# A decoder layer with a product-key expert mixer: tokens in two chunks, the second's dense layer written between the first's expert steps

## The chip, the cores and the metric

One core of one Trainium2 chip. The metric is the device time of one launch in microseconds, from runs of the whole kernel. "Span" is the time from the first to the last instruction in a profiled execution.

## The reference, cut to what matters

520 tokens (a prompt of 512 and 8 sample rows) pass one layer of width 1024. Its dense part is a conditioned norm, a recurrent branch (RG-LRU) beside windowed attention, a gated merge and a projection. Behind it stands the expert mixer: per token, 8 heads pick 16 of 16384 experts each, and for each expert one row of `u_tab` is dotted with the token and one row of `v_tab` is added with a weight.

```python
def layer(x, c, pos, conv_buf, h0, attn_fn, lp):
    ...
    hn = modulate(rmsnorm(x, lp['g_norm1']), sh1, sc1)
    z = hn @ lp['w_in']
    ...
    merged = jax.nn.sigmoid(gate_r) * y_r + jax.nn.sigmoid(gate_a) * y_a
    x1 = x + gt1[:, None, :] * (merged @ lp['w_out'])
    h2 = modulate(rmsnorm(x1, lp['g_norm2']), sh2, sc2)
    x2 = x1 + gt2[:, None, :] * peer(h2, lp['w_pq'], lp['sub_keys'], lp['u_tab'], lp['v_tab'])

def peer(h, w_pq, sub_keys, u_tab, v_tab):
    ...
        u = jnp.take(u_tab, ec, axis=0)
        act = jax.nn.gelu(jnp.einsum('cd,ced->ce', hc, u).astype(jnp.float32), approximate=False)
        wgt = (gc * act).astype(hc.dtype)
        vr = jnp.take(v_tab, ec, axis=0)
        return jnp.einsum('ce,ced->cd', wgt, vr)
```

A row of either table is 1024 float32, 4 KB. 128 tokens x 128 experts x 4 tiles, twice, and one group more for the sample rows: 65 groups of 8 u and 8 v gathers, each of 128 rows.

## The kernel before, in words

Each engine has its own program; semaphores order them, and each engine works through its program in order. There are two parts, one after the other.

**The dense layer** runs over all 520 tokens, as two halves of 260 columns (`HALF`). TensorE works off a list of "products" (`_plan`, L85 to L149), each into one of four accumulators of two PSUM banks. Most weights come in units of 1 MB into a ring of three (`load`, L406, on SP's queue). A weight block of 128 columns is used as a pair: ScalarE rounds it (`split_until`, L794), GpSimd subtracts to get the rest (L1460), and `project_split` (L505 to L515) does three matmuls for each piece of the contraction, 48 for a block: 24 for each half. Two rounded blocks fit at a time (`NHI`), so a rounding waits for the product two before it to end. `modulation` (L522 to L529) takes 24 units of 1 MB with 9 columns. The recurrence, the softmax and the merges stand on VectorE and ScalarE between them. At the end `keys` (L699 to L713) gives the scores for the experts.

**The experts** follow. VectorE's `topk` (L1332) finds a head's 16 indices and weights. A group is one half of a head, eight experts for each of 128 tokens, 64 groups (`GROUPS`) and one for the sample rows. For each group GpSimd issues eight gathers from `u_tab` and then eight from `v_tab` (`group`, L1446 to L1454), each of 128 rows into one of eight buffers; a u gather waits until VectorE has read the buffer (`s_urd`), a v gather until TensorE has (`s_vrd`). VectorE dots each u row with the token (`dot_products`, L1392 to L1397), ScalarE makes eight diagonal matrices of the weights (`weights`, L985 to L997), and TensorE adds up the v rows with them (`expert_sums`, L717 to L724). Tiles and heads are hardware loops (`Fori`). GpSimd's first gather waits until its last weight block is split, and VectorE, TensorE and ScalarE start on the experts once the dense layer is done. After each tile `finish` (L1399) adds the residual and norms the row.

Of the kernel before, what the change touches and what calls it, by code (L numbers as in the profile page):

```python
# [18 lines left out]
HALF = N // 2  # L29
# [18 lines left out]
SLOT = 8  # L48

# [22 lines left out]
RING = 3  # L72
UNIT = 2 * DC * P
NHI = 2
SPLIT = ("xr", "gr", "qk", "v", "gate_r", "gate_a", "attn", "out", "pq")
NACC = 4
STEPS = TILES * NKV
SAMPLE_STAGE = {0: 1, 2: 2, 3: 3}
UNIT_COLS = {"mod": UNIT, "xr": UNIT, "gr": UNIT, "band": 6 * P, "qk": UNIT, "v": UNIT, "gate_r": UNIT, "rnn": RC * P,
             "gate_a": UNIT, "attn": UNIT, "out": UNIT, "pq": UNIT, "keys": PH * NKEYS}  # L80
UNIT_NO, PRODUCT_NO, UNIT_READ = {}, {}, []
SPLIT_NO = {}


def _plan():  # L85
    def unit(name, i, *products):
        UNIT_NO[name, i] = len(UNIT_READ)
        UNIT_READ.append(0)
        if name in SPLIT:
            SPLIT_NO[name, 2 * i] = len(SPLIT_NO)  # L90
            SPLIT_NO[name, 2 * i + 1] = len(SPLIT_NO)
        for p in products:
            product(*p)
            UNIT_READ[-1] = len(PRODUCT_NO)

    def product(name, i=0, reads=None):
        PRODUCT_NO[name, i] = len(PRODUCT_NO)
        if reads:
            UNIT_READ[UNIT_NO[reads]] = len(PRODUCT_NO)

    for i in range(8):
        unit("mod", i, ("mod", i))
        if i == 3:
            product("norm", 0)
    for name, m in (("xr", 8), ("gr", 13)):
        for i in range(RC // 2):
            unit(name, i, (name, 2 * i), (name, 2 * i + 1))
            unit("mod", m + i, ("mod", m + i))
    for i in range(RC):
        unit("band", i, ("band", 2 * i), ("band", 2 * i + 1))  # L110
    for i in range(RC // 2):
        unit("qk", i, ("qk", 2 * i), ("qk", 2 * i + 1))
        unit("mod", 18 + i, ("mod", 18 + i))
        if i:
            product("turn", 2 * i - 2)
            product("turn", 2 * i - 1)
    unit("v", 0, ("v", 0), ("turn", RC - 2), ("turn", RC - 1), *[("v", t) for t in range(1, TILES + 1)])
    product("s", 0)
    product("sample", 0)
    unit("mod", 23, ("mod", 23))  # L120
    for i in range(STEPS):
        product("t", i)
        if i + 1 < STEPS:
            product("s", i + 1)
        if i in SAMPLE_STAGE:
            product("sample", SAMPLE_STAGE[i])
        product("o", i)
        c = i // 2
        if i % 4 == 0:
            unit("gate_r", c // 2)  # L130
        if i % 2 == 0:
            product("gate_r", c, ("gate_r", c // 2))
        else:
            unit("rnn", c, ("rnn", c))
    for i in range(DC // 2):
        unit("gate_a", i, ("gate_a", 2 * i), ("gate_a", 2 * i + 1))
        unit("attn", i, ("attn", 2 * i), ("attn", 2 * i + 1))
    for i in range(DC // 2):
        unit("out", i, ("out", 2 * i), ("out", 2 * i + 1))
    product("norm", 1)  # L140
    for i in range(2 * (TILES + 1)):
        product("rows", i)
    product("spread")
    for q in range(2):
        for i in range(4 * q, 4 * q + 4):
            unit("pq", i, ("pq", 2 * i), ("pq", 2 * i + 1))
        unit("keys", q, *[("keys", 2 * t + q) for t in range(TILES + 1)])
    for name, i in (("gt2", 0), ("gt2", 1), ("y", 0)):
        product(name, i)  # L149
# [40 lines left out]
def peer_program(nc, X, Wd, O):  # L190
    ctx = ExitStack()
    with ctx:
# [563 lines left out]
        def _(act):  # L756
# [51 lines left out]
            def two(a):  # L808
                return a[:, :, 0:HALF]
# [794 lines left out]
```

## Time and profile before

| | |
|---|---|
| runs, median of 3 | 2475.72 us (2469.61 to 2476.45) |
| profiled execution, span | 2483.4 us |
| busy, share of the span | TensorE 77%, VectorE 51%, ScalarE 28%, GpSimd 52% |
| first u gather issued | 903.87 us |
| u gathers / v gathers | 520 / 520 |
| moved by GpSimd's queue | 545.33 MB |
| moved by the other queue | 89.24 MB |

The profiled execution's own time is its span; no other time of it is given. Busy shares are means over two parts with different limits, so the parts are read apart. A busy TensorE means that matmuls are under way, not that they run at their peak.

### The profile page before, as it was taken

What the parts mean: (1) busy time and instruction counts of PE and PEld (TensorE: products, weight loads), DVE (VectorE), ACT (ScalarE), POOL (GpSimd) and SP (SyncE); (2) the same over time, 40 slices, a digit from 0 to 9 for tenths busy, and PEclk for the clock granted to TensorE, in tenths of its full rate; (3) what the DMA queues carried; (4) which work ended last, traced back from release to release, by engine and by line L of the source; (5) the groups of instructions that cost most, each with busy time, mean ns of one, the idle gap of its engine ahead of it and who ended that gap; (6) DMA issues with size and microseconds to landing.
All of it is one profiled execution on the core that took longest, in us unless ns stands there. A gap on an engine that the chain in (4) does not pass through costs nothing.

```text
span 2483.4 us, 25659 instructions
## 1 busy us (share of the span) xinstructions
PE 1922.2 (77%) x8102; PEld 1260.9 (51%) x8102; DVE 1273.5 (51%) x2896; ACT 706.2 (28%) x1770; POOL 1287.2 (52%) x1126
## 2 busy tenths in 40 slices
PE   8899988999997986676667757757767666776676
PEld 8899888888997972232223323323223222332232
DVE  2430366434333107656656746655756655765663
ACT  1222422233223323323313323222313323323222
POOL 0221123001431346667676766767767667766663
PEclk8899988999998997888878878788888888878877
DMA  5233332112221238999999999999999998999996
GB/s 222 94 131 111 123 136 97 39 47 82 86 86 35 77 134 334 366 363 360 362 332 357 373 342 363 361 339 340 366 356 358 354 351 327 369 354 358 372 347 233
DMA packets 164900, 635.52 MB, mean 256 GB/s; under 512 B 18800, under 2 KB 19640, under 8 KB 156224
## 3 DMA queue, kind: packets, MB, share of 16 engines
q0 software_dynamic: 149760, 545.33, 58.7%
q1 hardware_dynamic: 15072, 89.24, 10.1%
q8 instruction: 49, 0.80, 0.1%
q14 instruction: 19, 0.16, 0.0%
HBM read 631.30 MB, written 5.20 MB: 256 GB/s over the span
## 4 chain that ended last, share of the span: by engine, by line
PE 41%; issue 19%; DVE 15%; POOL 8%; DMA 6%; another core or an unknown queue 5%; ACT 5%; POOLq 0%; DVEq 0%; ACTq 0%; SPq 0%
PE acc L722 9%; POOL arena L1443 8%; PE acc L512 6%; PE acc L513 6%; PE acc L514 6%; DVE arena L1396 6%; DMA arena<-in_u_tab,pku 5%; PE acc L528 4%; PE acc L496 3%; ACT arena L996 2%; PE acc L562 2%; ACT pk L991 1%; PE acc L631 1%; PE acc L649 1%
## 5 line engine op out<-in xcount | busy, mean ns | idle before, releaser
L722 PE MATMUL acc<-arena 128*128 128x512 f32 x2080 | 1048.5, 668 | 473.6 <-ACT arena L996 346.8
L722 PEld LDWEIGHTS acc<-arena 128*128 128x128 f32 x2080 | 442.8, 217 | 1080.7 <-issue 1078.9
L1396 DVE CUSTOM_DVE_ANT_0 arena<-arena 128x1024 f32<-128x1024 f32 x520 | 631.2, 1226 | 416.0 <-DMA arena<-in_u_tab,pku 378.4
L1443 POOL DMA_INDIRECT arena<-in_v_tab,pku x520 | 552.9, 1063 | 316.3 <-issue 157.6
L1443 POOL DMA_INDIRECT arena<-in_u_tab,pku x520 | 526.2, 1012 | 167.3 <-issue 152.2
L1460 POOL TENSOR_TENSOR w_lo<-arena,w_hi 128x1024 fp32r<-128x1024 f32 x80 | 194.6, 2437 | 682.1 <-ACT w_hi L794 682.1
L512 PE MATMUL acc<-h_hi,w_hi 128*128 128x260 f32 x992 | 292.7, 295 | 22.0 <-DVE h_lo L1101 11.7
L513 PE MATMUL acc<-h_lo,w_hi 128*128 128x260 f32 x992 | 287.9, 290 | 0.0
L514 PE MATMUL acc<-h_hi,w_lo 128*128 128x260 f32 x992 | 287.1, 289 | 0.0
L988 ACT ACTIVATE pk<-pk 128x8 f32<-128x8 f32 x65 | 13.6, 209 | 936.3 <-issue 617.6
L512 PEld LDWEIGHTS acc<-h_hi,w_hi 128*128 128x128 f32 x992 | 194.4, 196 | 25.7 <-DVE h_lo L1101 12.6
L513 PEld LDWEIGHTS acc<-h_lo,w_hi 128*128 128x128 f32 x992 | 194.3, 196 | 2.0 <-issue 1.9
L514 PEld LDWEIGHTS acc<-h_hi,w_lo 128*128 128x128 f32 x992 | 194.2, 196 | 0.0
L794 ACT CAST w_hi<-arena 128x1024 fp32r<-128x1024 f32 x80 | 83.1, 1048 | 358.1 <-PE acc L514 325.4
L996 ACT ACTIVATE arena<-const,pk 128x128 f32<-128x128 f32 x520 | 158.8, 387 | 7.1
L528 PE MATMUL acc<-small,arena 128*128 128x9 f32 x768 | 111.6, 288 | 6.4 <-DMA arena<-w_mod 6.4
L528 PEld LDWEIGHTS acc<-small,arena 128*128 128x128 f32 x768 | 112.0, 236 | 6.4 <-issue 6.3
L991 ACT ACTIVATE pk<-pk 128x1 f32<-128x1 f32 x520 | 103.6, 281 | 2.1
L1349 DVE MAX8 pk<-arena 128x8 f32<-128x128 f32 x132 | 38.8, 294 | 76.7 <-ACT arena L966 53.9
L496 PE MATMUL acc<-arena 128*128 128x260 f32 x320 | 72.0, 385 | 0.0
L496 PEld LDWEIGHTS acc<-arena 128*128 128x128 f32 x320 | 61.4, 192 | 13.4 <-issue 4.4
L1077 DVE TENSOR_TENSOR mod<-acc,par 128x18 f32<-128x18 f32 x24 | 4.0, 176 | 116.7 <-PE acc L528 116.4
(230 smaller groups left out, 1863.0 us busy)
## 6 DMA issues: line engine op xcount, KB each, us to landing
arena<-w_mod SPq DMA_DIRECT2D x24, 1024.0 KB, 4.9
arena<-in_u_tab,pku POOLq DMA_INDIRECT x520
arena<-in_v_tab,pku POOLq DMA_INDIRECT x520
arena<-w_pq SPq DMA_DIRECT2D x8, 1024.0 KB, 4.7
arena<-w_xr SPq DMA_DIRECT2D x5, 1024.0 KB, 4.9
arena<-w_gr SPq DMA_DIRECT2D x5, 1024.0 KB, 4.9
arena<-w_qk SPq DMA_DIRECT2D x5, 1024.0 KB, 4.7
arena<-w_rnn SPq DMA_DIRECT2D x8, 640.0 KB, 4.0
```

Of the source, the lines that this page charges most:

```text
L496: mm = pe.matmul(a[:, h, 0:HALF], w[:, k, :], rhs[:, k, h * HALF:(h + 1) * HALF], start=(k == 0), stop=(k == ks - 1))
L512: pe.matmul(a[:, h, 0:HALF], w1[:, k, :], hi[k][:, cols], start=(k == 0), stop=False)
L513: pe.matmul(a[:, h, 0:HALF], w1[:, k, :], lo[k][:, cols], start=False, stop=False)
L514: mm = pe.matmul(a[:, h, 0:HALF], w2[:, k, :], hi[k][:, cols], start=False, stop=(k == DC - 1))
L528: mm = pe.matmul(a[:, c, 0:NCOND], w[:, c, k, :], cond[:, k, :], start=(k == 0), stop=(k == DC - 1))
L722: mm = pe.matmul(y[:, h, :], diag[q][:, j, :], vt_row[j][:, h * 512:(h + 1) * 512], start=False, stop=True, skip_group_check=True)
L794: act.copy(w_hi[n % NHI], half_unit(name_n, c_n)).then_inc(s_hi, 1)
L991: ins = act.activation(wcol[q][:, j:j + 1], gl[:, j:j + 1], ACT.Copy, scale=g[:, j:j + 1])
L996: ins = act.activation(diag[q][:, j, :], basis, ACT.Copy, scale=wcol[q][:, j:j + 1])
L1396: dve.tensor_tensor_reduce(u_row[j], u_row[j], hcur, 1.0, 0.0, ALU.mult, ALU.add, dots[q][:, j:j + 1]).then_inc(s_urd, 1)
L1443: pool.indirect_dma_start(out=row, out_offset=None, in_=table, in_offset=bass.IndirectOffsetOnAxis(ap=idx, axis=0), **more).then_inc(signa ...
L1460: pool.tensor_tensor(lo, half_unit(name, c), hi.bitcast(F32), ALU.subtract).then_inc(s_lo, 1)
```

## The change

Tokens come in two chunks, 256 and 264 columns (256 and the 8 sample rows). The first chunk's dense layer runs alone up to its first `keys` product (`PEER_FROM`). From there the kernel goes in 66 steps: step g holds VectorE's dots of group g and TensorE's sums of group g - 1. Each step has four quarters (`PARTS`). What is left of the dense work is cut into pieces by planned costs, one piece behind each quarter of steps 0 to 34 (`_limits`): 381.5 us of planned cost in steps 0 to 29, 32.2 in steps 30 to 34; 413.2 lie before `PEER_FROM`. Every engine's dense program is a generator that is run up to the quarter's limit (`Course`). All weights but the modulation's are loaded and split once for each chunk, in pieces of 128 columns; four piece buffers and two rounded ones serve the second chunk (eight and four before the first v gather, whose buffers they borrow). Accumulators are six of one bank, and the expert sums have a pair to themselves. Rows and scores of both chunks pass through DRAM (`spill`), loaded again by SP when a step wants them. Loops over tiles and heads are written out. Indices and weights have three buffers, and a head's choice stands two groups ahead.

GpSimd's order in a step is eight u gathers of group g, eight v gathers of group g - 1, then all weight splits of the step. `ROUND_AT` names for each weight block the product whose end lets ScalarE round it; GpSimd's split follows. In steps 1 to 29 the last such product lies in the fourth quarter except in steps 13, 16, 18 and 20 (third), 11, 14, 19, 26 and 29 (second) and 5 (none); in steps 30 to 32 in the fourth, in 33 and 34 there is none.

```diff
+CT = 2
+CP = CT * P
+W = CP + NB
+TOK = (CP, W)
...
+OWN, EXTRA = 4, 4
+OWN_HI, EXTRA_HI = 2, 2
+NACC = 6
...
+    def split(ch, name, c):
+        product(ch, name, c, ((name, c),), 2.9)
...
+PEER_FROM = NO[0, "keys", 0] + 1
...
+        over = max(free[p], HI_AFTER[p])
+        m = min([m for m in points if m + 1 >= over]) if n >= OWN_HI + EXTRA_HI else -1
...
+PARTS = 4
+HALF_WAY = NO[1, "keys", KEYS_B - 1] + 1
+HALF_STEP = 2 * PH * CT - 2
+LAST_STEP = HALF_STEP + 5
...
+    for (lo, hi), steps in (((PEER_FROM, HALF_WAY), HALF_STEP), ((HALF_WAY, NPRODUCTS), LAST_STEP - HALF_STEP)):
+        total, spent, at = sum(COST[lo:hi]), 0.0, lo
+        for i in range(steps * PARTS):
+            goal = total * (i + 1) / (steps * PARTS)
+            while at < hi and spent + COST[at] / 2 <= goal:
+                spent += COST[at]
+                at += 1
+            limits.append(hi if i == steps * PARTS - 1 else at)
...
+        class Course:
...
+            def until(self, limit):
+                while self.at < limit:
+                    self.at = next(self.steps, NPRODUCTS)
...
         @block.tensor
...
+            def expert_sums(g, js):
...
+                if js[0] == 0:
+                    pe.wait_ge(s_diag, g + 1)
...
+                for j in js:
+                    pe.wait_ge(s_vt[j], 16 * (g + 1))
...
+            course = Course(dense())
+            course.until(PEER_FROM)
+            for g in range(GROUPS + 2):
+                for q in range(PARTS):
+                    if g:
+                        expert_sums(g - 1, (2 * q, 2 * q + 1))
+                    if g * PARTS + q < len(LIMITS):
+                        course.until(LIMITS[g * PARTS + q])
...
         @block.scalar
...
+            def round_pieces(product):
...
+                while split[0] < len(SPLITS) and ROUND_AT[split[0]] <= product:
+                    piece = SPLITS[split[0]]
+                    src = await_piece(act, piece)
+                    if HI_AFTER[piece]:
+                        act.wait_ge(s_ready, HI_AFTER[piece])
+                    act.copy(w_hi[HI_SLOT[piece]], src[:, 0:D]).then_inc(s_hi, 1)
...
+            for g in range(GROUPS + 2):
...
+                if g:
+                    weights(g - 1)
+                for q in range(PARTS):
...
+                    if g * PARTS + q < len(LIMITS):
+                        course.until(LIMITS[g * PARTS + q])
...
         @block.vector
...
+            for g in range(GROUPS + 2):
+                tile, step = divmod(g - 1, 2 * PH)
+                for q in range(PARTS):
+                    if g <= GROUPS:
+                        dot_products(g, (2 * q, 2 * q + 1))
...
+                    if q == 1 and g % 2 == 0 and g // 2 + 1 <= HEADS:
+                        choose(g // 2 + 1)
...
+                    if g * PARTS + q < len(LIMITS):
+                        course.until(LIMITS[g * PARTS + q])
...
         @block.gpsimd
...
+            def gather_u(g, j):
...
+                if g:
+                    pool.wait_ge(s_urd, SLOT * (g - 1) + j + 1)
+                gather(u_row[j], X["u_tab"], indices(g, j), s_u[j], {})
...
+            def gather_v(g, j):
...
+                else:
+                    pool.wait_ge(s_vrd, SLOT * (g - 1) + j + 1)
...
+            def dense():
+                for n, p in enumerate(SPLITS):
+                    yield max(ROUND_AT[n], 0)
+                    hi, lo = w_hi[HI_SLOT[p]], w_lo[PIECE_SLOT[p]]
+                    pool.wait_ge(s_hi, n + 1)
+                    pool.tensor_tensor(lo, ring[PIECE_SLOT[p]][:, 0:D], hi.bitcast(F32), ALU.subtract).then_inc(s_lo, 1)
...
+            for g in range(GROUPS + 2):
+                if g <= GROUPS:
+                    for j in range(SLOT):
+                        gather_u(g, j)
+                if g:
+                    for j in range(SLOT):
+                        gather_v(g - 1, j)
+                for q in range(PARTS):
+                    if g * PARTS + q < len(LIMITS):
+                        course.until(LIMITS[g * PARTS + q])
```

## Rows read from the trace of the kernel before

**Rows 1.** The page, busy tenths of the span in 40 slices of 62 us.

```profile
PE   8899988999997986676667757757767666776676
...
DMA  5233332112221238999999999999999998999996
...
GB/s 222 94 131 111 123 136 97 39 47 82 86 86 35 77 134 334 366 363 360 362 332 357 373 342 363 361 339 340 366 356 358 354 351 327 369 354 358 372 347 233
```

**Rows 2.** Windows: us; busy of PE, PEld, DVE, ACT, POOL; PEclk, DMA, GB/s.

```profile
616.00:709.00 93.00, 91.33 (x760) 91.12 (x758) 39.02 (x47) 20.84 (x24) 37.81 (x16) 1.00 0.27 92
...
903.00:2460.00 1557.00, 1063.51 (x2177) 454.40 (x2178) 963.36 (x2249) 443.22 (x1325) 1079.12 (x1040) 0.83 0.94 352
...
1050.00:1100.00 50.00, 33.64 (x64) 14.05 (x64) 30.61 (x71) 14.46 (x52) 33.59 (x35) 0.79 0.97 375
...
1700.00:1750.00 50.00, 37.13 (x73) 15.86 (x73) 32.97 (x82) 15.21 (x45) 34.62 (x32) 0.83 0.91 333
```

**Rows 3.** Timeline of POOL at the first gathers: start us, us, what, idle before.

```profile
903.87 1.11 POOL L1443 DMA_INDIRECT arena<-in_u_tab,pku  x1 [9.00 <-DVE carrier L1388]
...
912.74 0.93 POOL L1443 DMA_INDIRECT arena<-in_u_tab,pku  x1 [0.31 <-issue]
...
921.14 0.94 POOL L1443 DMA_INDIRECT arena<-in_v_tab,pku  x1 [7.46 <-PE acc L728]
```

**Rows 4.** Timeline of the last group and the last store.

```profile
2434.06 0.93 POOL L1443 DMA_INDIRECT arena<-in_u_tab,pku  x1 [0.31 <-issue]
...
2481.21 0.32 SPq L471 DMA_DIRECT2D out_ys<-arena  x1
```

**Rows 5.** Timeline of DVE, a head's first and last index step.

```profile
850.27 0.29 DVE L1349 MAX8 pk<-arena 128x8 f32<-128x128 f32 x1 [53.92 <-ACT arena L966]
...
859.96 0.17 DVE L1376 CAST pku<-pk 128x16 uint32<-128x16 f32 x1
```

**Rows 6.** The chain that ended last: start us, us, what.

```profile
70.22 4.89 DVE h_lo L1101 x8
...
88.61 3.47 PE acc L528 x32
...
409.98 6.63 PE acc L603 x32
...
1160.46 5.25 DMA arena<-in_v_tab,pku
...
986.90 6.40 DMA arena<-in_u_tab,pku
...
1771.38 7.43 DMA arena<-in_u_tab,pku
```

**Rows 7.** Timeline of PE, two groups of expert sums.

```profile
1323.85 16.14 PE L722 MATMUL acc<-arena 128*128 128x512 f32 x32 [7.77 <-remote]
...
2459.80 14.79 PE L722 MATMUL acc<-arena 128*128 128x512 f32 x32 [0.23 <-ACT arena L996]
```

**Rows 8.** Timeline of ACT and POOL, one weight piece rounded and split.

```profile
620.88 1.05 ACT L794 CAST w_hi<-arena 128x1024 fp32r<-128x1024 f32 x1 [7.73 <-PE acc L514]
...
622.01 2.39 POOL L1460 TENSOR_TENSOR w_lo<-arena,w_hi 128x1024 fp32r<-128x1024 f32 x1 [9.24 <-ACT w_hi L794]
```

**Rows 9.** Timeline of ACT and PE, from a group's dots to its sums.

```profile
1342.26 0.21 ACT L988 ACTIVATE pk<-pk 128x8 f32<-128x8 f32 x1 [11.89 <-DVE pk L1396]
...
1344.20 2.44 ACT L996 ACTIVATE arena<-const,pk 128x128 f32<-128x128 f32 x8
...
1346.78 3.78 PE L722 MATMUL acc<-arena 128*128 128x512 f32 x4 [6.79 <-ACT arena L996]
```

**Rows 10.** The page, a DMA queue (packets, MB, share) and an issue group.

```profile
q1 hardware_dynamic: 15072, 89.24, 10.1%
...
arena<-w_mod SPq DMA_DIRECT2D x24, 1024.0 KB, 4.9
```

**Rows 11.** Timeline of POOL, a gather that took twice as long.

```profile
931.70 1.99 POOL L1443 DMA_INDIRECT arena<-in_u_tab,pku  x1 [0.30 <-issue]
```

More of the change, by code:

```diff
@@ L454, in _ @@
[L454 to L467 removed]
+            order = list(PIECES)
@@ new lines, in dense @@
+            def dense():
+                pe.wait_ge(s_cond, 1)
+                for i in range(8):
+                    yield NO[0, "mod", i]
+                    modulation(i)
+                    if i == 3:
+                        yield NO[0, "norm", 0]
+                        first_norm(0)
+                for ch in range(2):
+                    yield from chunk(ch)
+            def expert_sums(g, js):
+                tile, part, first, last = group_of(g)
+                if js[0] == 0:
+                    pe.wait_ge(s_diag, g + 1)
+                    if first and tile:
+                        pe.wait_ge(s_yfree, tile)
+                for j in js:
+                    pe.wait_ge(s_vt[j], 16 * (g + 1))
@@ new lines, in dense @@
+            def dense():
+                act.wait_ge(s_c, 16)
+                act.activation(cond, cT, ACT.Sigmoid).then_inc(s_sig0, 1)
+                act.wait_ge(s_par, 16)
+                first_norm_squares(0)
+                act.wait_ge(s_lam, 1)
+                act.activation(lamt[:, 1, :], lamt[:, 0, :], ACT.Exp, scale=-1.0).then_inc(s_elam, 1)
+                yield NO[0, "norm", 0]
+                root(0, 0)
+                for ch in range(2):
+                    yield from chunk(ch)
@@ new lines, in dense @@
+            def dense():
+                link(dve.memset(st_conv, 0.0))
+                dve.wait_ge(s_c, 16)
+                dve.wait_ge(s_sig0, 1)
+                dve.tensor_tensor(cond, cond, cT, ALU.mult).then_inc(s_cond, 1)
+                dve.wait_ge(s_par, 16)
+                decay_rates()
+                for i in range(4):
+                    yield NO[0, "mod", i]
+                    modulation(i)
+                yield NO[0, "norm", 0]
+                scale_rows(0, 0, xT, xT, rstd)
+                for i in range(4, 8):
+                    yield NO[0, "mod", i]
+                    modulation(i)
+                for i in range(8 - NACC, 8):
+                    await_read(dve, 0, "mod", i)
+                gains(0, prm("g1"))
+                modulate(0, 0, xT)
+                for ch in range(2):
+                    yield from chunk(ch)
@@ L1439, in _, with settled, gather @@
+            final_norm(TILES - 1)
+            add_residual(TILES)
+            final_norm(TILES)
         @block.gpsimd
         def _(pool):
-            def gather(row, table, idx, signal, read=None):
-                more = {} if read is None else {"engine_sem": read}
+            def settled():
+                pool.sem_inc(s_passed, 1)
+            def gather(row, table, idx, signal, more):
+                settled()
                 pool.indirect_dma_start(out=row, out_offset=None, in_=table,
@@ L1467, in _, with indices @@
[L1467 to L1475 removed]
+            def indices(g, j):
+                if g == GROUPS:
+                    return eidx_s[:, j:j + 1]
+                col = g % 2 * SLOT + j
+                return eidx[g // 2 % 3][:, col:col + 1]
@@ L1479 @@
+            course = Course(dense())
+            course.until(PEER_FROM)
+            for g in range(GROUPS + 2):
[5 more added lines that the diff above has]
+                        gather_v(g - 1, j)
+                for q in range(PARTS):
+                    if g * PARTS + q < len(LIMITS):
+                        course.until(LIMITS[g * PARTS + q])
 def kernel(**inputs):
```

2319 lines of the change are left out of this document (1318 added, 1001 removed).

## The prediction

> **What bounds the kernel now.** I read the page's busy tenths first: the span has two halves. Up to slice 14 TensorE is at 8 or 9 tenths and the DMA engines mostly idle; from slice 15 the DMA engines are at 9 and TensorE at 6 or 7 [rows 1]. The windows give sizes: in the dense layer TensorE is busy 91.3 of 93 us, in the experts the DMA engines are busy 0.94 of the time at 352 GB/s [rows 2]. The dense half runs to the first gather at 903.9 [rows 3], and 64 groups of 16 gathers begin between there and 2434.1 [rows 4], one in 23.91 us; the last takes 49.3 more to the end at 2483.4. A group is 16 x 128 rows of 4 KB, 8.39 MB, so its floor is 22.4 us at the best rate shown, 375 GB/s, and 25.2 at the worst, 333 [rows 2]. Laying the idle DMA under the busy TensorE is thus worth looking for: half the dense layer beside half the experts.
>
> **What the change adds up to.** I split the new order in four: first chunk alone, steps that hold dense work, plain steps, tail.
>
> *First chunk alone.* Before, dense products begin at 75.1, when the last rest is written [rows 6]; the first chunk's rows are half as wide, so I take 70. From 75 to 903.9 are 828.8 us, with 16 modulation units of 3.47 [rows 6], 55.5 in all; 773 are left, half of which is 387. Of this the second half of pq now comes after the first gather: 8 products of 24 matmuls at 91.33/760 = 0.120 us [rows 2], 23 us. The modulation comes back whole, 55.5, and a head's choice of indices costs 860.1 - 850.3 = 9.9 [rows 5]. 70 + 387 - 23 + 55.5 + 9.9 = 499; the sample rows' attention, one piece of which is 6.6 [rows 6], goes with the second chunk, so I take 490. The ends: 455 if only the plan's costs count (413 to that point, with the idle of the start), 530 if every gap is paid whole.
>
> *The chain of a step with dense work.* GpSimd's program in step g is: eight u of group g, eight v of group g - 1, then every weight split that the plan puts in step g. A split waits for ScalarE's rounding, which waits for a product to end that TensorE works off in step g, and TensorE puts two rows' sums of group g - 1 ahead of each quarter's products. So the v rows of group g cannot be asked for until TensorE is nearly through step g, and TensorE cannot begin step g + 1 until they land. From GpSimd's start of a step:
> - eight u gathers at (912.74 - 903.87)/7 = 1.27 us each [rows 3], then the first v is issued at 10. It lands 5.25 to 7.43 us after its issue, with a full queue [rows 6]: at 15.3 to 17.4. I take 16.
> - TensorE: eight rows of sums take 16.1 us after 7.8 us of idling, 14.8 after a short gap [rows 7]. It will have idled longer than 7.8, so I take 16.1. Dense products beside them: the plan's 381.5 us over 30 steps, 12.7 a step; its 2.9 for a product agrees with 24 x 0.120 = 2.88 [rows 2]. Together 28.8.
> - the last split: the cast begins at 620.88, the split ends at 624.40 [rows 8], 3.5; with a signal and the next issue, 3.9.
>
> Sum: 16 + 28.8 + 3.9 = 48.7 us when the last rounding of the step hangs on a product of its last quarter. From the plan's limits and rounding points, written out, that is so in 19 of steps 1 to 29. In four (13, 16, 18, 20) it hangs on the third quarter, 3.4 + 3.2 earlier: 42.1. In six it hangs on the second or there is none; then ScalarE sets the period, since the weights of the next group stand behind its dense work: an eviction of 0.6, a table load of 1.3 and 1342.26 to 1346.78 = 4.5 [rows 9] behind TensorE's 28.8: 35.2. Steps 30 to 34 hold 6.4 us of dense: three of 16 + 22.5 + 3.9 = 42.4, two of 22.5 + 6.4 = 28.9. Together 19 x 48.7 + 4 x 42.1 + 6 x 35.2 + 3 x 42.4 + 2 x 28.9 = 1490. Step 0 has no v and waits for u, dots and a choice: 20.
>
> VectorE's additions (dots twice two, a choice of 9.9 every second step, its dense pieces) fill some 20 us of such a step and lie beside TensorE. SP's queue carries the second chunk's weights and the spilled rows: at most 89.2 MB less the 25.2 of modulation [rows 10], 64 MB, 1.9 per step, 5 us of DMA time that falls where the gathers have drained. Both cost nothing as long as the step is this long. If the cover goes, those 5 us join the step: 170 in all, which would only add to a step that is already long. The loops written out and the accumulators of one bank instead of two I put at nothing; no row prices them, and what they can give is bounded by the 1.5 us by which a plain step of before exceeds its floor, what they can cost by the first chunk's range.
>
> A gather into an empty queue has no row here. The Trainium skill (DMA: Bandwidth & Descriptors, Anatomy of one DMA) puts a GpSimd DMA at 2.0 us plus its bytes at 436 GB/s, 3.2 us for such a row, as an estimate; the rows above say 5.25 at the least. By the page the v rows would land 2 us earlier in some 30 steps, and the sum would be 60 us lower.
>
> *Plain steps and tail.* Steps 35 to 63 have no splits; u and v gathers queue behind each other as before, 29 x 23.91 = 693, between 22.4 and 25.2 each [rows 2]. The last group and the end: 49.3. Together 743.
>
> 490 + 20 + 1490 + 743 = 2743 of span, against 2483.4. That span lies 7.7 above the median of the runs shown, 2475.72; I take the 7.7 off: **2735**, slower by 10.5%. In short, 34 dense steps of 43.8 us cost more than 34 plain steps and the dense work in a row: 34 x 23.91 + 414 = 1227.
>
> Own range: the landing of v, 1.2 either way in 26 steps, 31; sums at 14.8, 44 less; first chunk 35 less or 40 more; plain steps 43 less or 38 more; attention steps 10 to 15, where VectorE's choice stands ahead of a softmax, up to 60 more. Not all at one end: 2600 to 2870.
>
> **Rivals.**
> - *The last split never sets the step* (faster). If splits come out early everywhere, each step is TensorE's 28.8 with ScalarE's 6.4: 29 x 35.2 + 5 x 28.9 = 1165, so 490 + 20 + 1165 + 743 - 8 = 2410. For it: six steps are like that already. Against: GpSimd's order leaves no way round. It decides from a mean step of (2483.4 - 490 - 20 - 743)/34 = 36.2 us downward. Chance 0.10.
> - *Full overlap, the DMA engines bound* (faster): (8.39 + 1.9)/0.352 = 29.2 a step, 993 for 34, in all 2238. For it: DMA idles in the dense half. Against: the same order, and TensorE alone needs 28.8. Chance 0.05.
> - *No overlap at all*: the products run in gaps, 1227 for the 34 steps, in all 2472; no change that can be told. Chance 0.04.
> - *GpSimd's head of a step is slow*: gathers of 1.99 us beside VectorE's work do occur, against 0.94 [rows 11, 4]. At 1.99 + 0.3 the first v is issued at 18.3 instead of 10; 8.3 us in 26 steps is 216: 2950. Against: in the 1557 us of the experts GpSimd was busy 1079 for 1040 gathers [rows 2], 1.04 each, so few are slow. The Trainium skill (SBUF — State Buffer, SBUF: two separate sides) has VectorE's two-port copies lock GpSimd out of writing descriptors, and the second chunk brings such copies beside the gathers. Chance 0.08.
>
> **How the numbers follow.** The forecast's mechanism has 0.73. A measurement of this kernel tells about 0.3% from no change, 7 us. Slower by more: 0.73 + 0.08, less a little for the near end, 0.80. Faster: 0.10 + 0.05 and a share of the in-a-row case, 0.17. Same: 0.03. The range leaves out the faster cases and the far part of the slow head: 2580 to 2910.
>
> **What would show it.** Right: in the dense steps, u gathers bunch right behind a split and the DMA share falls to near 0.5 to 0.65 there, with TensorE idle some 16 us behind each bunch, waiting for a v row; steps of 40 to 49 us up to step 30 and near 24 from step 35; first gather near 490. Wrong in the chain: v rows already landed when TensorE begins its sums, steps of 29 to 36 us, DMA share over 0.85. Wrong in size: a first gather beyond 530, gathers near 2 us, or TensorE waiting for softmax rows in steps 10 to 15.

## The result and the profile after

The changed kernel takes 3040.55 us (median of four runs, 3024.30 to 3049.53) against 2472.66 of the kernel before beside it: a ratio of 1.2286, interval 1.2240 to 1.2331. Slower, as forecast, but by more than twice as much: 2735 was given, with 2910 as the upper end. The profiled execution has a span of 3047.7 us. Line numbers below are those of the changed kernel.

The page of the changed kernel: busy tenths in 40 slices of 76 us, one DMA queue (packets, MB, share), and groups of instructions (busy us, mean ns, idle time before them and what ended most of it).

```profile
PE   7978997364665555564657474664666666565666
...
DMA  5444453556755645646565656576789888888886
...
q1 hardware_dynamic: 53136, 158.16, 15.5%
...
L1031 PE MATMUL y<-arena 128*128 128x512 f32 x2080 | 1068.9, 671 | 996.3 <-DMA arena<-in_v_tab,pku 932.8
...
L1890 POOL TENSOR_TENSOR w_lo<-arena,w_hi 128x1024 fp32r<-128x1024 f32 x160 | 386.2, 2416 | 1018.6 <-ACT w_hi L1064 1018.6
...
L1858 POOL DMA_INDIRECT arena<-in_u_tab,pku x520 | 581.0, 1117 | 317.8 <-DVE pk L1749 158.9
```

In [rows 1] one of the two was at 8 or 9 tenths nearly everywhere. Here, from slice 9 to 28, TensorE is at 4 to 7 tenths and the DMA engines at 4 to 7 as well. TensorE and GpSimd, which issues the gathers, wait for each other: over the whole span TensorE idles 996 us ahead of the expert sums, 933 of them ended by v rows, and GpSimd idles 1019 us ahead of splits, all for ScalarE's rounding (653 and 647 of these in steps 1 to 34, as lines further down show). The second chunk fetches the weights again: 158 MB on SP's queue against 89 in [rows 10].

Windows of the changed kernel: us, busy of PE, PEld, DVE, ACT and POOL, granted clock, DMA share, GB/s. They are the first chunk from 100 us on, steps 1 to 34, and steps 35 to 63.

```profile
100.00:547.60 447.60, 386.54 (x2582) 366.61 (x2581) 175.75 (x388) 179.87 (x337) 162.43 (x70) 0.87 0.44 145
577.50:2201.20 1623.70, 932.78 (x3930) 599.62 (x3930) 694.37 (x1579) 405.20 (x1029) 786.18 (x630) 0.78 0.61 216
2201.20:2983.30 782.10, 478.46 (x984) 204.64 (x985) 424.02 (x1035) 185.14 (x601) 512.11 (x465) 0.80 0.86 319
```

The same view of the kernel before, its dense layer from 100 us on.

```profile
100.00:904.00 804.00, 760.73 (x5430) 718.67 (x5429) 274.53 (x568) 238.38 (x416) 198.66 (x79) 0.94 0.24 86
```

From the issue of each step's first u gather the span divides as the forecast's sum did:

| term | forecast, us | measured, us | more |
|---|---|---|---|
| first gather | 490 | 547.6 | 58 |
| step 0 | 20 | 30.0 | 10 |
| 34 steps with dense work | 1490 | 1623.7 | 134 |
| 29 plain steps | 693 | 782.1 | 89 |
| last group to the end | 49.3 | 64.4 | 15 |
| span | 2743 | 3047.7 | 305 |

The timeline of the changed kernel: the first gather; step 24, from its first u gather to that of step 25, on all engines; then a pair of plain steps (43 and 44). Columns: start, us, what, idle before and what ended it.

```profile
547.57 1.09 POOL L1858 DMA_INDIRECT arena<-in_u_tab,pku  x1 [11.41 <-DVE pku L1795]
...
1733.11 0.97 POOL L1858 DMA_INDIRECT arena<-in_u_tab,pku  x1 [0.15 <-issue]
...
1743.61 0.94 POOL L1858 DMA_INDIRECT arena<-in_v_tab,pku  x1 [0.30 <-issue]
...
1749.99 5.66 PE L1031 MATMUL y<-arena 128*128 128x512 f32 x8 [20.61 <-DMA arena<-in_v_tab,pku]
...
1778.55 1.04 ACT L1064 CAST w_hi<-arena 128x1024 fp32r<-128x1024 f32 x1 [4.37 <-PE acc L749]
...
1779.67 2.34 POOL L1890 TENSOR_TENSOR w_lo<-arena,w_hi 128x1024 fp32r<-128x1024 f32 x1 [4.78 <-ACT w_hi L1064]
...
1782.15 0.95 POOL L1858 DMA_INDIRECT arena<-in_u_tab,pku  x1
...
2421.46 0.94 POOL L1858 DMA_INDIRECT arena<-in_u_tab,pku  x1 [0.30 <-issue]
...
2429.29 0.17 DVE L1795 CAST pku<-pk 128x16 uint32<-128x16 f32 x1
2429.37 1.22 DVE L1749 CUSTOM_DVE_ANT_0 arena<-arena 128x1024 f32<-128x1024 f32 x1
...
2431.41 1.14 POOL L1858 DMA_INDIRECT arena<-in_u_tab,pku  x1 [9.01 <-DVE pk L1749]
2432.85 1.99 POOL L1858 DMA_INDIRECT arena<-in_u_tab,pku  x1 [0.30 <-issue]
```

Step 24 is the forecast's chain, link by link: eight u issues (10.5 us), the v row 6.4 after its issue, TensorE idle for 20.6 until then, 28.6 to the last rounding, 3.6 to the next step's first u. In all 49.0 us, against the forecast's 16 + 28.8 + 3.9 = 48.7.

The plain steps show something that the forecast did not have. In step 43 GpSimd issues four u gathers and then stands for 9.0 us. It waits for dot product 4 of the even step before, whose row it is to overwrite, and that dot product stands behind the choice of the next head's indices, whose last step is the row at 2429.29. In the kernel before GpSimd's order was the same, eight u and then eight v, but the choice stood behind all eight dot products of a group; the last of them and the first row of the choice:

```profile
1739.17 1.23 DVE L1396 CUSTOM_DVE_ANT_0 arena<-arena 128x1024 f32<-128x1024 f32 x1
...
1740.32 0.29 DVE L1349 MAX8 pk<-arena 128x8 f32<-128x128 f32 x1
```

The change put it between dot products 3 and 4. So the steps alternate: the 15 odd ones take 33.2 us on average, the 14 even ones 20.3, in the mean 26.97 where the kernel before takes 23.91, and the DMA share is 0.86 instead of 0.94 [rows 2].

### The profile page after: what moved, and what is told of

The parts are those of the page before. It is cut to its first block, busy times and chain, and to the rows that moved or that the text cites. A ratio compares the mean times of both kernels' runs of the same rounds, so it can differ in the third digit from the quotient of the medians.

```text
span 3047.7 us, 25065 instructions
## 1 busy us (share of the span) xinstructions
PE 1934.2 (63%) x8078; PEld 1279.1 (42%) x8078; DVE 1349.7 (44%) x3142; ACT 807.5 (26%) x2040; POOL 1513.2 (50%) x1206
## 3 DMA queue, kind: packets, MB, share of 16 engines
q0 software_dynamic: 149760, 545.33, 48.7%
q8 instruction: 64, 1.05, 0.1%
## 4 chain that ended last, share of the span: by engine, by line
issue 23%; PE 15%; DVE 13%; DMA 8%; POOL 8%; another core or an unknown queue 4%; ACT 2%; POOLq 0%; DVEq 0%; ACTq 0%
PE y L1031 10%; POOL arena L1858 6%; DVE arena L1749 5%; DMA arena<-in_v_tab,pku 5%; DMA arena<-in_u_tab,pku 3%; POOL w_lo L1890 2%; PE acc L749 1%; PE acc L747 1%; PE acc L748 1%; DVE pku L1770 1%; DVE pk L1778 1%; DVE pku L1779 1%; DVE pk L1769 1%; ACT w_hi L1064 1%
## 5 line engine op out<-in xcount | busy, mean ns | idle before, releaser
L1031 PE MATMUL y<-arena 128*128 128x512 f32 x2080 | 1068.9, 671 | 996.3 <-DMA arena<-in_v_tab,pku 932.8
L1031 PEld LDWEIGHTS y<-arena 128*128 128x128 f32 x2080 | 440.7, 218 | 1545.4 <-issue 1491.9
L1890 POOL TENSOR_TENSOR w_lo<-arena,w_hi 128x1024 fp32r<-128x1024 f32 x160 | 386.2, 2416 | 1018.6 <-ACT w_hi L1064 1018.6
L1858 POOL DMA_INDIRECT arena<-in_u_tab,pku x520 | 581.0, 1117 | 317.8 <-DVE pk L1749 158.9
L1064 ACT CAST w_hi<-arena 128x1024 fp32r<-128x1024 f32 x160 | 167.2, 1046 | 1042.1 <-PE acc L749 696.4
L747 PE MATMUL acc<-h_hi,w_hi 128*128 128x256 f32 (+1 forms) x992 | 319.5, 322 | 14.8 <-DVE h_lo L1420 14.8
L749 PE MATMUL acc<-h_hi,w_lo 128*128 128x256 f32 (+1 forms) x992 | 288.4, 291 | 0.7 <-issue 0.7
L748 PE MATMUL acc<-h_lo,w_hi 128*128 128x256 f32 (+1 forms) x992 | 288.6, 291 | 0.0
L1296 ACT ACTIVATE pk<-pk 128x16 f32<-128x16 f32 x33 | 10.1, 307 | 404.5 <-DVE pk L1782 321.5
L1427 DVE SCALAR_TENSOR_TENSOR arena<-arena,par 128x256 f32<-128x256 f32 x60 | 49.0, 817 | 78.9 <-ACT arena L1186 76.9
```

What stands on the lines that cost most here:

```text
L747: pe.matmul(a[:, 0:n], w1[:, k, :], hi[k][:, 0:n], start=(k == 0), stop=False)
L748: pe.matmul(a[:, 0:n], w1[:, k, :], lo[k][:, 0:n], start=False, stop=False)
L749: mm = pe.matmul(a[:, 0:n], w2[:, k, :], hi[k][:, 0:n], start=False, stop=(k == DC - 1))
L1031: mm = pe.matmul(y[:, h, :], diag[g % 2][:, j, :], vt_row[j][:, h * 512:(h + 1) * 512], start=(first and j == 0), stop=True, skip_group_ch ...
L1064: act.copy(w_hi[HI_SLOT[piece]], src[:, 0:D]).then_inc(s_hi, 1)
L1858: pool.indirect_dma_start(out=row, out_offset=None, in_=table, in_offset=bass.IndirectOffsetOnAxis(ap=idx, axis=0), **more).then_inc(signa ...
```

## The experiments

All kernels do the same arithmetic as the changed kernel and change only who issues or computes what, and when; in e0 and e10 the second chunk's dense layer moves as a whole. In each, "dense" is the mean of steps 1 to 34 and "plain" that of steps 35 to 63, from the issue times of the first u gathers. The kernel before, run beside each, took 2473 to 2491 us; so kernels of different rows are best compared by their ratios. Where the splits are on VectorE, GpSimd's line numbers are 19 higher and the other engines' 1 higher than in the changed kernel.

| kernel | median, us | ratio to before | dense | plain |
|---|---|---|---|---|
| the change | 3041 | 1.2286 (1.2240 to 1.2331) | 47.8 | 27.0 |
| e0: dense layer in series | 2825 | 1.1376 (1.1326 to 1.1427) | 26.1 | 25.9 |
| e10: in series, choice last | 2657 | 1.0672 (1.0608 to 1.0735) | 23.6 | 23.9 |
| e4: choice last | 2930 | 1.1781 (1.1730 to 1.1833) | 47.4 | 23.9 |
| e1: v first | 2871 | 1.1531 (1.1464 to 1.1598) | 42.5 | 27.4 |
| e3: splits on VectorE | 2781 | 1.1201 (1.1146 to 1.1255) | 40.9 | 25.8 |
| e5: gathers by quarter | 2643 | 1.0622 (1.0566 to 1.0678) | 38.6 | 23.9 |
| e8: by quarter, choice last | 2630 | 1.0580 (1.0525 to 1.0635) | 37.8 | 25.1 |
| e7: as e8, splits on VectorE | 2626 | 1.0561 (1.0508 to 1.0614) | 37.8 | 25.0 |
| e9: v first, splits on VectorE, choice last | 2584 | 1.0392 (1.0330 to 1.0454) | 37.5 | 23.7 |
| e13: as e8, early weights | 2490 | 0.9980 (0.9950 to 1.0010) | 33.9 | 25.0 |
| e14: as e11, v and u in turn | 2478 | 0.9978 (0.9944 to 1.0011) | 33.8 | 24.7 |
| e11: as e9, early weights | 2459 | 0.9850 (0.9818 to 0.9882) | 34.1 | 23.7 |

**Does the overlap pay at all?** e0 runs every engine's dense course to its end ahead of the first gather (the same line on all five engines).

```
-            course.until(PEER_FROM)
+            course.until(NPRODUCTS)
```

> The second chunk's dense layer runs wholly before the first gather instead of between the experts. Theory (each of the 34 dense steps pays some 16 us in which TensorE waits for v rows, because GpSimd issues them only behind the step's splits): the overlap costs more than it hides. First chunk 548, second chunk alone 34 x 12.7 = 432 of TensorE plus some idle, say 470, step 0 30, 63 steps at the measured 26.97 = 1699, end 64: 2811 (2750 to 2870), less than the 3040 of the changed kernel. Rival (the dense work of the second chunk is itself slow, with two rounded-weight buffers and four pieces): it takes 1624 - 34 x 26.97 = 707 alone, and the time stays at 3000 or above.

It took 2825 us, 14 from the theory's number: side by side in this order, the two kinds of work take some 220 us longer than one behind the other (1.2286 against 1.1376 times before). The window of its second chunk:

```profile
547.00:1089.00 542.00, 443.84 (x2979) 404.79 (x2978) 234.38 (x473) 223.46 (x412) 211.50 (x88) 0.92 0.36 121
```

TensorE's own dense work is 443.8 us, near the forecast's 34 x 12.7 = 432; in the other 98 it idles, some 12 of them at the end, behind its last product. The number agrees with the theory partly by luck: the chunk took 71 us more than the 470 assumed, and the 63 steps 26.0 instead of 26.97.

**The choice.** e4 moves it to the end of an even step, and what hangs on it on ScalarE and VectorE into the odd step. The edit on VectorE; ScalarE's exponentials go to the first quarter of the odd step in the same way:

```
-                    if q == 0:
-                        if g % 2 and (g + 1) // 2 <= HEADS:
-                            shares((g + 1) // 2)
+                    if q == 2 and g % 2 and (g + 1) // 2 <= HEADS:
+                        shares((g + 1) // 2)
+                    if q == 0:
...
-                    if q == 1 and g % 2 == 0 and g // 2 + 1 <= HEADS:
+                    if q == 3 and g % 2 == 0 and g // 2 + 1 <= HEADS:
                         choose(g // 2 + 1)
```

> The top-16 choice of the next head moves on VectorE from between dot products 3 and 4 of an even step to behind dot product 7; the exponentials and the shares move to the odd step. Theory: in the steps without dense work the last four u gathers no longer wait for it, the two kinds of step (33.4 and 20.2 us) become alike, and 29 of them fall from 26.97 to 24: 2955 (2930 to 2980). Rival (the wait only moves to the other kind of step): 3025 to 3055.

Plain steps fell to 23.90, what they were before the change, and 2930 is the lower end of the expected range. By the spans of the two traces the gain is 114 us: 89 in the plain steps, 12 in step 0 (17.7 instead of 30.0) and 12 in the 34 dense ones. Its window over steps 36 to 63, to be read against the third row of the changed kernel's windows:

```profile
2209.00:2871.00 662.00, 456.45 (x903) 189.86 (x904) 414.61 (x988) 173.66 (x564) 475.77 (x448) 0.84 0.96 361
```

The DMA share is back at 0.96. Together with the series this prices the two chunks alone:

> The second chunk's dense layer wholly before the first gather, and the choice behind dot product 7. Theory: 64 steps without dense work at 24 in place of 25.8 to 27; what is left over the kernel before is then the price of two chunks in the dense layer, 1089 against 904: 2690 (2660 to 2720). Rival (the slower steps come from the new order of the gathers and not from the choice): 2790 or above.

e10 took 2657, with plain steps as before. Its first gather is the row

```profile
1085.80 1.09 POOL L1858 DMA_INDIRECT arena<-in_u_tab,pku  x1 [22.37 <-DVE pku L1795]
```

against 903.87 in [rows 3]: 182 us for doing the dense layer in two halves, and its span is 176 above before's. So the change is made of three pieces, by medians: two chunks, 2484 to 2657; the choice between the dots, to 2825; and an overlap that takes longer than the series, to 3041. The prices hold in this order only: inside the overlap the choice costs 110 (e4), in the series 168.

**Which hold on GpSimd?** The forecast's theory was that v rows are asked for too late because GpSimd works through one list: u, v, splits. Three kernels each take one hold away. e1 exchanges the two loops:

```
+                if g:
+                    for j in range(SLOT):
+                        gather_v(g - 1, j)
                 if g <= GROUPS:
                     for j in range(SLOT):
                         gather_u(g, j)
-                if g:
-                    for j in range(SLOT):
-                        gather_v(g - 1, j)
```

> At the head of a step GpSimd issues the eight v gathers first and the eight u gathers behind them; nothing else moves. Theory: the first v row lands some 6.5 us after the head instead of 16 to 18, so TensorE starts 10 us earlier in the some 28 dense steps that it waits for v in: 2760 (2700 to 2830). Rival (the order in which GpSimd issues them does not set the step: the u rows are late instead, or the weights are): 2990 or above.

2871: neither number. In the 14 steps in which TensorE's first sum waited for v, the row was used 4.2 to 4.55 us after the head of the step, where step 24 above shows 16.9; but only 170 of the expected 280 us came back. Its waits from 550 to 1950 us (total, times, longest):

```profile
DVE arena L1749 <- DMA arena<-in_u_tab,pku: 434.9, 31, 40.0
...
PE y L1031 <- ACT arena L1319: 173.4, 13, 23.0
...
PE y L1031 <- DMA arena<-in_v_tab,pku: 129.2, 14, 14.0
```

The same view of the changed kernel, steps 1 to 34:

```profile
PE y L1031 <- DMA arena<-in_v_tab,pku: 652.8, 31, 41.8
POOL w_lo L1890 <- ACT w_hi L1064: 646.6, 84, 34.8
...
DVE arena L1749 <- DMA arena<-in_u_tab,pku: 331.3, 73, 40.2
...
ACT w_hi L1064 <- DMA arena<-w_gate_r: 111.2, 5, 44.7
```

The wait for v fell from 653 to 129 us, but u now came late, as the rival has it: VectorE's dot products waited 435 in place of 331, and behind them ScalarE's weights, for which TensorE stood 173. In place of 10 us a dense step gained 5.3.

e3 takes the splits of the second chunk from GpSimd and puts them into VectorE's course, each at the product at which the plan has it:

```
+            def late_splits():
+                for n in range(EARLY, len(SPLITS)):
+                    yield ROUND_AT[n]
...
+                    dve.wait_ge(s_hi, n + 1)
+                    dve.tensor_tensor(w_lo[PIECE_SLOT[p]], ring[PIECE_SLOT[p]][:, 0:D], w_hi[HI_SLOT[p]].bitcast(F32),
+                                      ALU.subtract).then_inc(s_lo, 1)
...
-            course = Course(dense())
+            course = Course(merged())
```

> The splits of the second chunk's weights (w minus its rounded part) are made by VectorE in its own course; GpSimd only gathers from the first step on. Theory: GpSimd then waits only for free rows, v is there when TensorE comes to it, and a dense step is TensorE's 28.8 us plus some 4 to 6 of hand-offs: 34 x 34 = 1156 in place of 1624, 2575 (2500 to 2680). Rival (the splits on VectorE stand behind dot products that wait for u rows, so the chain only changes its engine): 2900 or above.

2781: a gain of 260, not of 460. GpSimd no longer waits for splits; its waits from 550 to 1950 us:

```profile
POOL arena L1877 <- DVE pk L1750: 639.0, 75, 28.9
...
PE y L1032 <- DMA arena<-in_v_tab,pku: 286.9, 23, 45.6
```

It now waits 639 us with a u gather for a dot product, with the v gathers queued behind. That is a hold of the same kind, one place further on.

e5 leaves all work where it is, and takes the gathers from the head of a step. In each quarter of step g GpSimd issues two v of group g and two u of group g + 1, whose buffers were set free one quarter earlier, and then makes that quarter's splits (the eight u of group 0 come ahead of step 0):

```
+                for q in range(PARTS):
+                    h, r = divmod(g * PARTS + q - 1, PARTS)
+                    if 0 <= h <= GROUPS:
+                        for j in (2 * r, 2 * r + 1):
+                            gather_v(h, j)
+                        for j in (2 * r, 2 * r + 1):
+                            if h < GROUPS:
+                                gather_u(h + 1, j)
                     if g * PARTS + q < len(LIMITS):
                         course.until(LIMITS[g * PARTS + q])
```

> One edit alone: GpSimd issues two v and two u gathers in each quarter, one quarter behind the sums and dot products that free the rows, in place of eight and eight at the head of the next step; its splits and the choice stay as they are. Theory: this alone takes the wait for v rows out of the dense steps, which fall from a mean of 47.8 to some 37, and the choice still costs what the run with the choice alone gave back, some 110: 2740 (2690 to 2790). Rival (the gain of the kernel with both edits came from the choice in the dense steps too): 2850 or above.

2643, some 400 us less by one edit, and better than expected by 100. Of these some 310 are in the 34 dense steps, and some 90 in the plain ones, where the choice no longer holds up the v gathers. The waits of the dense steps, 550 to 1750 us:

```profile
PE y L1031 <- ACT arena L1319: 267.3, 26, 43.9
...
POOL w_lo L1890 <- ACT w_hi L1064: 244.1, 34, 24.1
```

A wait of TensorE for v is no longer among them. The expectation was wrong in its second half: the choice costs nothing here, as plain steps of 23.9 say; eight u gathers no longer stand in one block ahead of the v gathers. e8, which moves the choice as well, agrees:

> As the kernel with two v and two u gathers in each quarter and the choice behind dot product 7, but GpSimd keeps the splits. Theory (what costs is that the v rows of a group are asked for behind the last split of the step before, not who makes the split): v is asked for three quarters of a step ahead of its sums, and dense steps fall to some 37: 544 + 30 + 34 x 37 + 29 x 24 + 62 = 2590 (2500 to 2680). Rival (GpSimd's own time for gathers and splits in one order is the bound, or the gathers in between hold up the splits that TensorE waits for): 2750 or above.

Its interval overlaps that of e5, at 1.058 and 1.062: dense steps gain 0.8 us and plain steps lose 1.2. Against e4, which has the choice in the same place, it shows what the order of the gathers alone is worth: 300 us. And e7, with the splits on VectorE besides, was meant to be compared with v first (e9):

> GpSimd issues two v and two u gathers in each quarter of a step, one quarter behind the sums and dot products that free the rows, in place of eight and eight at the head; splits on VectorE and the choice behind dot product 7. Theory: once GpSimd makes no splits, neither place holds up v, and the time is that of the kernel with v first, within 60 us (2450 to 2600). Rival (u and v coupled quarter by quarter, each waits for the slower of VectorE's dots and TensorE's sums): 80 us or more above it.

e7 is 0.2% from e8. So when the order is mended, it does not matter that GpSimd makes the splits: what cost 300 us was where they stood in its list, not the 2.4 us that each takes. Against e9, the next kernel, e7 is 42 us slower, which its theory allowed; most of it is in the plain steps (25.0 against 23.7), which hold no splits.

**The next wait.** e9 has all three single edits:

> Three edits together: v gathers ahead of u gathers at the head of a step, the second chunk's splits on VectorE, the choice behind dot product 7. Theory (each removed a different hold on GpSimd's gathers: its own splits, the u gathers in front, the choice in front of dots): GpSimd asks for each v row as TensorE frees it, TensorE no longer waits for v, and a dense step is 28.8 of TensorE plus 5 to 7 of hand-offs: 544 + 20 + 34 x 35 + 29 x 24 + 62 = 2512 (2450 to 2600). Rival (with the splits VectorE's course is the bound and GpSimd waits for its dot products, as in 639 us of the run with the splits there alone): dense steps stay near 40 and the time at 2650 or above.

2584; dense steps of 37.5 where 35 was expected, and neither of the rival's waits. From 550 to 1750 us:

```profile
POOL arena L1877 <- PE y L1032: 513.4, 163, 16.1
...
PE y L1032 <- ACT arena L1320: 216.8, 22, 23.5
```

GpSimd now waits for TensorE, which is as it should be, and TensorE for the diagonal weights of the group: ScalarE makes them at the start of a step, behind its dense work of the step before. e11 makes them in the last quarter of the group's own step, ahead of that quarter's dense work:

```
-                if g:
-                    weights(g - 1)
                 for q in range(PARTS):
...
                     if q == 3:
+                        if g <= GROUPS:
+                            weights(g)
```

> As the kernel with v first, splits on VectorE and the choice last, and ScalarE builds the diagonal weights of group g in the last quarter of step g, ahead of that quarter's dense work, instead of at the start of step g + 1. Theory: TensorE's wait for those weights (217 us in the 1200 us of the dense steps) was the next to end last; two thirds of it go: 2584 - 150 = 2434 (2380 to 2500), about the kernel before or faster. Rival (ScalarE now waits for the step's last dot products ahead of dense work that TensorE needs, or v rows come late again): 2540 or above.

2459, where the kernel before took 2491 beside it: faster by 1.5% (interval 0.9818 to 0.9882). The page, busy tenths in slices of 62 us:

```profile
PE   8896999865878767888798887888757666675775
...
DMA  6443445528887786889869998998999999999996
```

From slice 11 to 28 TensorE and the DMA engines are both at 6 to 9 at the same time. The wait for weights, 560 to 1650 us, is

```profile
PE y L1032 <- ACT arena L1320: 120.4, 21, 22.2
```

The same edit in e8 gave e13:

> The same early weights in the kernel with gathers by quarter, the choice last and the splits still on GpSimd. Theory: as there, 2630 - 150 = 2480 (2420 to 2540). Rival (GpSimd's splits between the gathers take the place of the wait for the weights): 2590 or above.

2490, level with the kernel before, with GpSimd's splits in place. Its dense steps are as short as e11's, 33.9 against 34.1; it loses in the plain ones, 25.0 against 23.7. The last try went after the 120 us:

> As the fastest kernel so far (splits on VectorE, the choice last, early weights), but each v gather is followed by the u gather of the same row number instead of eight v and then eight u. Theory: six of the eight u rows are asked for some 10 us earlier, so the dot products and the weights that TensorE still waits for (120 us in the dense steps) come earlier; a third of that goes: 2459 - 40 = 2419 (2390 to 2450). Rival (v gathers now stand behind u gathers that wait for VectorE's dot products, as in the kernel with gathers by quarter, which was 42 us slower than the one with v first): 2475 or above.

```
                 for j in range(SLOT):
                     if g:
                         gather_v(g - 1, j)
                     if g < GROUPS:
                         gather_u(g, j)
```

2478, as its rival had it: level with the kernel before, where e11 was 1.5% faster. The dense steps gained nothing (33.8 against 34.1), and their waits say why:

```profile
PE y L1032 <- ACT arena L1320: 144.6, 22, 22.0
POOL arena L1877 <- DVE pk L1750: 140.1, 32, 12.9
```

A v gather stands again behind a u gather that waits for VectorE, and the wait for the weights did not shrink. The loss itself is in the plain steps, 24.7 instead of 23.7; what makes it was not tried.

## Why the prediction was right or wrong

The forecast was right in its sign and in its chain for a dense step, and wrong in its sum, three terms of which were too small: the dense steps by 134 us, the plain steps by 89 and the first chunk by 58. Step 0 adds 10, which e4 gives back, and the end 15, for which no run was made.

**The sign and the mechanism held.** "the v rows of group g cannot be asked for until TensorE is nearly through step g, and TensorE cannot begin step g + 1 until they land": the waits show 653 us of it, step 24 shows its links within a microsecond each, the DMA share of 0.61 lies in the forecast's 0.5 to 0.65, and undoing only this order, from e4 to e8, gives 300 us back. Of the 19 steps put at 48.7 us, six took 49.0 to 50.6 and the middle one 52.4.

**The first chunk was halved where half does not hold.** "773 are left, half of which is 387" took TensorE's gaps as half as long for half the rows. The two windows from 100 us on give 804 - 760.7 = 43 us of idle time before and 447.6 - 386.5 = 61 after. Of the 61, 7 are the end of the choice, behind TensorE's last product at 540.3, which the forecast priced by itself; 54 are gaps, in place of 22: 32 of the 58 us. Dense products also begin at 77.6 where 70 was taken. Most of the rest is busy time, at a granted clock of 0.87 where it was 0.94. The end of 530, "if every gap is paid whole", was too low: the gaps did not stay, they grew, presumably since half as many rows cover half as much of the next product's preparation. The second chunk by itself (e0) shows the same with 86 of its 98 us. No run tried to shorten them.

**The plain steps were priced as before, and VectorE's order was not.** "Steps 35 to 63 have no splits; u and v gathers queue behind each other as before, 29 x 23.91". The order of the gathers was as before; the place of the choice on VectorE was not. With it between dot products 3 and 4, the fifth u gather of the next group waits for it, and the v gathers stand behind that. The bounds of 22.4 and 25.2 came from DMA rates alone and left out that GpSimd can stop issuing; the measured 26.97 is outside. The row was there to be read: a choice of 9.9 us [rows 5] was written down as work of VectorE "beside TensorE", and who waits for VectorE's dot products, the u gathers, was not asked. e4 shows that this is the whole 89 us.

**The dense steps: right in kind, 134 us too short.** TensorE's work was not the cause: it was busy 932.8 us in the 34 steps, and the sum took 961 (413.7 of products and 34 x 16.1). The waits were longer. The forecast had 26 steps in which TensorE idles 16 + 3.9 = 19.9 us for v, 517 in all; it did so in 31, for 21.1 on average, 653. After four of the six steps priced at 35.2, since their last rounding comes early (11, 19, 26, 29), it still waited 10.8 to 15.8 us for v, where 6.4 for weights had been assumed.

The classes came out at 54.4 for 48.7 (19 steps), 44.3 for 42.1 (four), 38.5 for 35.2 (six), 44.4 for 42.4 (three) and 23.9 for 28.9 (two). The six come near by luck: step 5 took 23.1, and step 19 took 56.0, the largest miss of all. Five others, 1, 6, 10, 15 and 27, took 58.7 to 67.5 and make half of the 134. The forecast's "up to 60 more" for attention steps went into its own range but not into the sum.

And "Both cost nothing as long as the step is this long", said of VectorE and of SP's queue, failed. ScalarE waited 111 us for pieces of gate_r in steps 15 to 19, five times, up to 44.7, and 23 for one of gate_a in step 20; these six steps are 50 us above their prices. Each such piece loads into one of four slots once a product has freed it, so the load stands in the chain ahead of the rounding. In step 19, which begins at 1476.6, the load was issued 48.4 us after the head, and the last rounding began 52.4 after it:

```profile
1525.02 0.33 SPq L544 DMA_DIRECT2D arena<-w_gate_r  x1
...
1529.03 1.04 ACT L1064 CAST w_hi<-arena 128x1024 fp32r<-128x1024 f32 x1 [44.70 <-DMA arena<-w_gate_r]
```

The product that freed the slot was late too. The sample rows' attention ahead of it, planned at 2.0 us, took 9.7, and the product itself 5.6 instead of 2.9, at a granted clock of 0.50, the level of 1.2 GHz (windows as above):

```profile
1509.70:1519.40 9.70, 9.70 (x134) 9.50 (x133) 0.00 (x0) 0.00 (x0) 0.00 (x0) 0.78 0.01 4
1519.40:1525.00 5.60, 5.60 (x26) 5.60 (x26) 2.93 (x7) 0.00 (x0) 0.00 (x0) 0.50 0.00 0
```

What these loads are worth in all was not tried; e11 still has 68 us of the wait for gate_r.

**The rivals.** "The last split never sets the step" was put at 35.2 a step and 2410 in all; with the order mended, steps of 34 us are what e11 shows, with the diagonal weights made early as well, and its 2459 lies above 2410 by somewhat less than what the first chunk was short. The slow head of GpSimd is out: u gathers took 1.12 us on average and v gathers 1.05, and in 31 of the 34 dense steps the first v was issued 10 to 12.5 us after the first u. "No overlap at all" was put at 2472; the series really costs 2825, since the two chunks and the choice between the dot products were not in that sum.

**The landing of v.** I took 6 us between 5.25 and 7.43. In the 31 dense steps in which TensorE's first sum waited for v, it began 5.86 to 10.03 us after the issue, 6.3 in the middle. The Trainium skill's rule (DMA: Bandwidth & Descriptors, Anatomy of one DMA) came to 3.2, as an estimate. In e1 v is issued 21 us or more behind the last gather; there it took 4.21 to 4.55 in 14 steps from the start of GpSimd's issue, and 3.26 to 3.58 from its end. So the trace is near the page's figure if the issue itself is left out, and 1.0 to 1.4 us above it otherwise. One of them, GpSimd's issue and TensorE's start:

```profile
1591.43 0.96 POOL L1858 DMA_INDIRECT arena<-in_v_tab,pku  x1
...
1595.97 4.53 PE L1031 MATMUL y<-arena 128*128 128x512 f32 x6 [8.26 <-DMA arena<-in_v_tab,pku]
```

## What to carry to other kernels

An engine that issues transfers in program order is a queue: for each transfer ask what stands in front of it, for what that waits, and whether the wait ends a whole step later than the buffer is free. Keep late work out of the list in front of it. Two ways did that here: each gather issued in the quarter in which its buffer comes free (300 us from e4 to e8), after which moving the splits off the engine was worth nothing more, or nothing but gathers in the list, v first (e9). And ask what a piece of work moved between others holds up: the choice in the middle of the dot products cost 110 us. Two things did not halve with the rows: the gaps between dependent products, and the loading, rounding and splitting of weights (160 splits in place of 80); price a second chunk by a series run (182 us here) before counting what it may hide.

## What the runs showed of the hardware

A gather of 128 rows of 4 KB issued 21 us or more behind the last one (e1) is used 4.2 to 4.55 us after its issue begins; behind eight others (the changed kernel) 6.3 in the middle.

Issues of a gather that take 1.99 us instead of 0.94 come where VectorE runs dot products, as at 2432.85 above: in nearly every odd plain step 3 to 5 of the 16 gathers take over 1.6 us, in all but one dense step 0 to 3. Each of the 108 gathers of the changed kernel over 1.6 us ran beside dot products for over half its time, and 652 of the 799 under 1.0 us beside none; but 55 that lay beside dot products for over nine tenths of their time stayed under 1.0 us too. The Trainium skill (SBUF — State Buffer, SBUF: two separate sides) says that VectorE and GpSimd share a port pair, which one instruction holds for its whole length, and names for VectorE two-port modes, with copies as the example, and instructions with two inputs in SBUF, these against a GpSimd instruction that reads SBUF. The dot products have two such inputs, and a copy ran beside two of the 108; so the trace points to the second kind, but no run tested the cause.

TensorE's clock after a wait, in windows of the fastest kernel (columns as above): the first eight sums after 12.35 us of idling took 6.77 us, the next eight 3.60.

```profile
1508.42 6.77 PE L1032 MATMUL y<-arena 128*128 128x512 f32 x8 [12.35 <-issue]
1516.77 3.60 PE L1032 MATMUL y<-arena 128*128 128x512 f32 x8
```

```profile
1508.40:1512.00 3.60, 3.58 (x5) 1.52 (x6) 3.40 (x10) 2.60 (x5) 0.00 (x0) 0.50 1.01 403
...
1516.80:1520.30 3.50, 3.50 (x11) 1.54 (x10) 2.90 (x8) 0.39 (x1) 1.95 (x2) 1.00 0.81 249
```

The granted clock was 0.50, the level of 1.2 GHz, and then 1.00, that of 2.4. This wait cost some 3 us beyond its own length.
